# Ring slots of the split weights: a displacement of its own for each of four slots

## What is computed

```python
def hybrid_layer(x, norm_g, w_in, b_merge, w_pa, w_pb, w_out):
    h = rmsnorm(x, norm_g)
    proj = jnp.einsum('bsd,dc->bsc', h, w_in)            # 512 x 1024 by 1024 x 6656
    a_qkv, z_a, b_qkv, z_b, r_a, r_b = jnp.split(proj, offs, axis=-1)
    ...                                                  # three dilated groups of 4 heads, 8 block-sparse heads
    y_a = jnp.einsum('bsc,cd->bsd', attn_a.astype(x.dtype) * jax.nn.silu(z_a), w_pa)
    y_b = jnp.einsum('bsc,cd->bsd', attn_b.astype(x.dtype) * jax.nn.silu(z_b), w_pb)
    merged = (jax.nn.sigmoid(r_a + b_merge[:D_MODEL]) * y_a
              + jax.nn.sigmoid(r_b + b_merge[D_MODEL:]) * y_b)
    return x + jnp.einsum('bsd,de->bse', merged, w_out)
```

## Time and profile before

| what | value |
|---|---|
| median of 3 runs | 453.0 us (452.82 to 454.27) |
| the profiled execution | 452.7 us |
| its span, first to last instruction | 450.9 us |
| TensorE, matmuls | busy 97% of the span |
| TensorE, weight loads | 84% |
| VectorE, ScalarE, GpSimd | 45%, 43%, 37% |
| DMA | mean 102 GB/s |
| granted TensorE clock | 1.000 (mean) |

### The profile page before, as it was taken

How to read it: one execution, slowest core, us unless ns; L and a number is a source line. 1 busy time by engine, 2 the same in 40 slices (tenths; PEclk the granted TensorE clock), 3 DMA queues, 4 the chain that set the end, 5 groups by cost and what they waited for, 6 DMA issues and landing times.

```text
span 450.9 us, 6290 instructions
## 1 busy us (share of the span) xinstructions
PE 437.5 (97%) x2417; PEld 378.7 (84%) x2417; DVE 204.6 (45%) x335; ACT 193.8 (43%) x392; POOL 168.1 (37%) x106
## 2 busy tenths in 40 slices
PE   8899999999999999999999999899999999999995
PEld 7689998899889988988778888688888888888885
DVE  3931244313203233668977757806107074083434
ACT  6743553345325453567446555323324353233111
POOL 3645332234243233655437552435434445300000
PEclk9999999999999999999999999999999999999999
DMA  8862352024302263034122022213322273320421
GB/s 289 272 186 94 95 140 94 2 94 136 98 1 96 94 166 106 11 106 139 50 94 93 1 70 92 73 57 121 103 72 93 93 256 101 135 93 0 138 96 47
DMA packets 39404, 46.21 MB, mean 102 GB/s; under 512 B 3640, under 2 KB 35408, under 8 KB 39376
## 3 DMA queue, kind: packets, MB, share of 16 engines
q1 hardware_dynamic: 36928, 45.62, 31.7%
q10 hardware_dynamic: 2448, 0.21, 0.4%
HBM read 39.48 MB, written 2.15 MB: 92 GB/s over the span
## 4 chain that ended last, share of the span: by engine, by line
PE 89%; DVE 7%; ACT 2%; issue 1%; DMA 1%; DVEq 0%; ACTq 0%
PE ps L740 18%; PE ps L744 18%; PE ps L741 18%; PE ps L784 4%; PE ps L786 4%; PE ps L785 4%; PE ps L945 3%; PE ps L944 3%; PE ps L943 3%; PE ps L840 3%; PE ps L887 3%; PE ps L860 3%; PE ps L877 2%; PE ps L843 2%; ACT squares L980 1%; DVE gat_lo L1261 1%
## 5 line engine op out<-in xcount | busy, mean ns | idle before, releaser
L668 POOL TENSOR_TENSOR w_lo<-raw,w_hi 128x1024 fp32r<-128x1024 f32 (+1 forms) x59 | 139.7, 2369 | 186.6 <-ACT w_hi L960 180.2
L740 PE MATMUL ps<-hT_hi,w_hi 128*128 128x512 f32 x336 | 135.6, 404 | 4.5 <-DVE zf L1226 2.0
L744 PE MATMUL ps<-hT_lo,w_hi 128*128 128x512 f32 x336 | 131.3, 391 | 0.0
L741 PE MATMUL ps<-hT_hi,w_lo 128*128 128x512 f32 x336 | 131.1, 390 | 0.0
L740 PEld LDWEIGHTS ps<-hT_hi,w_hi 128*128 128x128 f32 x336 | 63.2, 188 | 15.2 <-ACT w_hi L960 2.4
L744 PEld LDWEIGHTS ps<-hT_lo,w_hi 128*128 128x128 f32 x336 | 63.1, 188 | 13.6
L741 PEld LDWEIGHTS ps<-hT_hi,w_lo 128*128 128x128 f32 x336 | 63.3, 188 | 10.0
L960 ACT CAST w_hi<-raw 128x1024 fp32r<-128x1024 f32 (+1 forms) x59 | 60.1, 1019 | 19.2 <-PE ps L744 16.4
L784 PE MATMUL ps<-w_hi,hT_hi 128*128 128x256 f32 x160 | 45.9, 287 | 0.0
L786 PE MATMUL ps<-w_lo,hT_hi 128*128 128x256 f32 x160 | 44.7, 279 | 0.0
L785 PE MATMUL ps<-w_hi,hT_lo 128*128 128x256 f32 x160 | 44.7, 279 | 0.0
(11 more groups left out here) (140 smaller groups left out, 637.8 us busy)
## 6 DMA issues: line engine op xcount, KB each, us to landing
raw<-in_w_in SPq DMA_DIRECT2D x25, 1024.0 KB, 5.0
raw<-in_w_out SPq DMA_DIRECT2D x4, 1024.0 KB, 4.9
KTs<-KTs SPq DMA_DIRECT2D x12, 256.0 KB, 3.4
xs<-in_x SPq DMA_DIRECT2D x4, 512.0 KB, 4.8
raw<-in_w_pb SPq DMA_DIRECT2D x4, 512.0 KB, 4.1
res<-in_x SPq DMA_DIRECT2D x4, 512.0 KB, 4.0
out<-weighted SPq DMA_DIRECT2D x8, 256.0 KB, 2.2
raw<-in_w_in SPq DMA_DIRECT2D x2, 512.0 KB, 8.1
```

The source lines that it names most:

```text
L668: nc.gpsimd.tensor_tensor(ring(w_lo, n, kt), src, ring(w_hi, n, kt).bitcast(F32), ALU.subtract).then_inc(lo_ready, 1)
L740: pe.matmul(out, wh, hh, start=(k == 0), stop=False)
L741: pe.matmul(out, wl, hh, start=False, stop=False)
L744: return pe.matmul(out, wh, hl, start=False, stop=(k == kts - 1))
```

## The change

A table of four distances, in elements of 4 bytes, is added. Every step that is not a value step has its weights displaced by the entry of its slot: 16, 32, 48 and 96 bytes. Value steps keep their 32 bytes. The ring is long enough for it (slot 3 ends at element 4,184 of 4,224), and neighbouring slots overlap nowhere where they did not before. Both parts of the weights, `w_hi` and `w_lo`, follow the same function.

```diff
 NRING = 4
 SKEW = 8
 APART = 64
+SLOT_SKEW = [4, 8, 12, 24]
 RING = 2 * (2 * KT_D * P + APART)
...
         def ring_at(n):
 
-            return KT_D * P * (n % NRING) + APART * (n % NRING // 2) + (SKEW if step_kind(n) == "v" else 0)
+            return KT_D * P * (n % NRING) + APART * (n % NRING // 2) + (SKEW if step_kind(n) == "v" else SLOT_SKEW[n % NRING])
```

## The result

The changed kernel takes 460.5 us (458.24 to 461.32, 4 runs) against 453.6 us (452.82 to 455.17, 4 runs) beside it: a ratio of 1.0135, 95% interval 1.0108 to 1.0161. Forecast were 450.7 us and a range of 447.6 to 456.8 us. The change makes the kernel slower, by about three times what was forecast as a gain, and the time lies outside the range.

The account below looks back on a forecast made before the run. The prediction took TensorE's number of matmuls times their start-to-start distance as the bound. From 453.0 us it took 2.3 us (1,095 matmuls at 2.1 ns), giving 450.7 us, range 447.6 to 456.8 us.

Parts of the forecast that it names:

- The bound: Whole kernel: TensorE, busy 97% of the span; time is the number of matmuls times their start-to-start distance.
- The two reads meet: Every matmul: weight load and running matmul read SBUF together and hinder each other; surplus 13.3 ns level, 10.0 in value steps.
- The rule of the Trainium skill: All matmuls: loading the next weights takes no read bandwidth from the running matmul, so no displacement can do anything.
- The 16-byte cachelines: Displaced weights: all four distances are whole lines, so operands cover as many lines as before and the sum would be zero.
- The step that failed: Column and branch steps: the value step's -3.3 ns for 32 bytes taken as nearest row; mean gain 2.1 ns a matmul.
- paid per matmul and not per column: Undisplaced matmuls: the surplus over one column per cycle is 13.3 ns at both 512 and 256 columns.
- The shares of the slots: Ring slots 0 to 3: gains of 1.7, 3.3, 1.7 and 1.7 ns a matmul, mean 2.1 ns.
- What reaches the end: Affected projection matmuls: nearly all the gain counts, 1,095 of 1,152 matmuls at 2.1 ns, 2.3 us.
- its 57 matmuls: Affected matmuls before two TensorE waits for VectorE (221.00 and 287.25 us): their gain only lengthens the wait, so not counted.
- The writers' cost at nothing: Ring writers: ScalarE's copies stay 1.05 us and GpSimd's differences 2.40 us, so 16, 48 and 96 bytes cost nothing.
- The slower rival: Column and branch steps: displaced loads meet the stream more often, 5.0 ns lost each, 5.5 us, giving 458.5 us; chance 0.25.

Follow-up runs that it names:

- e6_lo_only: Kernel before the change with only w_lo displaced, by 32 bytes, outside value steps: column-step distances 239, 228 and 233 ns, 233.3 in the mean.
- e3_input32: Kernel before the change with everything from hT on 32 bytes further and weights unmoved, so column steps' moving operand alone is displaced: 233.3 ns there.
- e2_both32: Changed kernel with weights of all slots and everything from hT on 32 bytes further: column steps 226.7 ns, branch steps 233.3, value steps 119.8.
- e4_values0: Kernel before the change with value weights not displaced (SKEW 0 instead of 8): second value step 120.0 ns a matmul instead of 116.7.
- e10_fine: Changed kernel with 4, 8, 192 and 240 bytes in slots 0 to 3: steady distances 232.1, 230.8, 228.8 and 228.8 ns.
- e11_values0_timed: Kernel before the change with value weights undisplaced (SKEW 0), timed: 455.7 us (12 runs) against 454.4 (23 runs), ratio 1.0040.

## Why the prediction was wrong

**The bound** was read rightly. The kernel is a row of matmuls, and a change of their distance reaches the end: 5.4 us of 7.9 are that, in the trace of one execution.

**The two reads meet**: right as far as the addresses go. Surplus and displacement belong together (120.0 against 116.7 ns with `SKEW` undone), and it is the two operands' position to each other that counts (226.7 ns with both displaced, 233.3 with either alone). What happens inside such a meeting no run shows, and e6_lo_only doesn't fit a price for each meeting. The rule of the Trainium skill that was weighed against it ("TensorE: Matmul & The Clock Gate", "Step-by-step: what each phase is for": the next load takes no read bandwidth from the running matmul) would have made every displacement free. It does not hold so for these fp32r matmuls: moving the load's addresses alone takes the distance from 226.7 to 233.3 ns. Whether it is bandwidth that is lost there is not shown. The 16-byte cachelines of the Trainium skill, "SBUF — State Buffer" ("Specifications (TRN2)"), don't give the measure of it either: 16 bytes, a whole line, cost 6.6 ns, and 4 bytes already cost 5.4.

**The step that failed** is the one that took -3.3 ns from the value step, 256 columns wide, as the nearest row for matmuls of 512 columns. The four slots were to gain 2.1 ns in the mean; they lost 6.7 in the steady stretch. It is a matter of sign, not of size. With the moving operand 32 bytes off level, the surplus of a narrow matmul falls from 13.3 to 10.0 ns, and that of a wide one rises from 13.3 to 20.0. So the conclusion "paid per matmul and not per column" is true of level operands only. The prediction named two things in which the value step differs, its shape and its displaced side. It missed the third, the width, which decided: the output projection shows both signs in matmuls of the same tensors. That undisplaced matmuls of both widths have the same 13.3 ns had suggested that width does not matter, and that does not follow. The side, which it did name, decided nothing at 512 columns: 233.3 ns with either operand displaced.

**The shares of the slots** (half the gain at 16 bytes, and so on) fell with it. All four distances cost between 6.2 and 7.5 ns. For the narrow matmuls the guess that 16 bytes give half was close: 1.5 of 3.3 ns.

**What reaches the end.** With 6.7 ns for 1,095 matmuls the prediction's own sum would have been 7.3 us. Measured are 5.4 in the trace, and 5.4 between executions at full clock. The term that is too big is the body: the 648 matmuls ahead of 287 us lost 3.1 ns each. By the table above it is the matmuls in short rows, behind other work, that lost next to nothing. They had been off their steady 226.7 ns before, being such a place, and so had less to lose; why they are off it, no run separates. The waits gave back 0.3 us, near what the prediction took off for its 57 matmuls (0.4 us at 6.7 ns).

**The writers' cost at nothing**: right.

**The slower rival**, given 0.25, was the case that came true. It had two reasons. That the side counts, load against stream, is refuted at this width: displacing the stream instead costs the same 6.6 ns (e3_input32). That "the steady 226.7 ns looks like a state in which both fall into step" fits, since long rows lost nearly everything that was lost, but no run shows the step itself. Its price, half of the 10.0 ns of rows 8 and so 5.5 us, lies next to the measured 5.4 by luck: that place didn't change with the displacement (0.71 and 0.70 us), and 5.0 ns stands between a steady loss of 6.7 and one of 3.1 in the body. Its 458.5 us lay beyond the range from the start, because the range was cut at a mean of 3.5 ns, below that rival's own price.

**What stays open** is why a narrow matmul gains where a wide one loses, and what repeats every 256 bytes. One reading that the numbers allow: with the moving operand off level the surplus is 20.0 ns at 512 columns and 10.0 at 256, as if it were paid per column, while level it is the same 13.3 for both. Then loss would turn into gain near 340 columns, an estimate from these two widths (13.3 / 20.0 x 512). With the stationary operand off level it fits less well (20.0 and 11.8). Widths of 384 columns and others were not tried off level on their own.

## What to carry to other kernels

Look at the start-to-start distance of matmuls in a stretch without waits, for each width apart, and compare it with one column per cycle. A surplus that moves with addresses can be moved back. For rows of fp32r matmuls of 512 columns with a weight load each, keep stationary and moving operand at the same address modulo 256 bytes. One load of three off it costs as much as all three. A displacement that pays in one width is no evidence for another: try it there, in a different distance for each buffer, since one run then shows them all.

## What the runs showed of the hardware that I had not expected

- Some 6.7 ns, 3% of a 512-column matmul, hang on where two operands begin in SBUF, down to 4 bytes (232.1 ns). Level places found: 0 and 256 bytes (226.7); not 64 (233.3), 128 (232.5), 192 or 240 (228.8 both).
- A displacement of 32 bytes saves 1.5 to 3.3 ns in matmuls of 256 columns.
- With one of three loads off level the pattern of distances is 239, 228, 233 ns, with the mean of three off level.
- The loss belongs to long rows: with six or more of their kind directly ahead, wide matmuls lost 5.9 ns, and the first of a row lost 1.1.
- TensorE's granted clock fell to the 1.2 GHz level for a few microseconds in part of the executions, those of the kernel before among them, about 1.6 us of time each. In the changed kernel's trace it fell within 1 us after a wait of 1.8 us, and it did so at this place in four more of the 14 traces (e2_both32, e4_values0, e10_fine, e11_values0_timed). The other nine have a wait of 1.8 to 2.0 us there and no fall.
